# Two fused transformer blocks on one core: the second attention's steps taken one apart

## The reference

```python
# layer 1 of the second block
qkv = rmsnorm(x) @ w_qkv                      # 16 heads of 64, 4 key and 4 value heads
scores = einsum(q, k) / sqrt(64) + bias       # bias by distance, within 128 positions
probs = softmax(concat([scores, sink]))[..., :-1]
x = x + (probs @ v) @ w_o
# experts: per token and head, 16 of 128 keys on each of two sides, then 16 of the 256 pairs
sc = einsum((rmsnorm(x) @ w_q), subkeys)      # 8 heads, 2 sides
idx, g = best 16 pairs, softmax of their scores
h = x_norm . u_tab[idx];  a = g * gelu(h);  x = x + sum(a * v_tab[idx])
```

## Time and profile before

| what | value |
|---|---|
| median of three runs | 1950.23 us (1944.83 to 1954.89) |
| profiled execution | 1950.94 us, its span 1949.1 us |
| mean granted TensorE clock | 0.965 of full |
| TensorE busy | 1655.1 us (85%) |
| VectorE busy | 1049.2 us (54%) |
| ScalarE busy | 554.3 us (28%) |
| GpSimd busy | 587.3 us (30%) |
| moved by DMA | 639.39 MB, mean 328 GB/s |
| second expert loop | 1279.68 to 1949.10 us |

### The profile page before, as it was taken

How to read it: one execution, slowest core, us unless ns; L and a number is a source line. 1 busy time by engine, 2 the same in 40 slices (tenths; PEclk the granted TensorE clock), 3 DMA queues, 4 the chain that set the end, 5 groups by cost and what they waited for, 6 DMA issues and landing times.

```text
span 1949.1 us, 18676 instructions
## 1 busy us (share of the span) xinstructions
PE 1655.1 (85%) x6184; PEld 966.1 (50%) x6184; DVE 1049.2 (54%) x2676; ACT 554.3 (28%) x1664; POOL 587.3 (30%) x533
## 2 busy tenths in 40 slices
PE   7999999998779988787997868789898887777776
PEld 5888885885335544442543335544454443333232
DVE  2212202123676666676766643466677767677664
ACT  1211000101333433333333323243333343333432
POOL 1000000001344543344444420123344444444442
PEclk9999999999899999999999988789999999999999
DMA  8545241565999999999999982579999999999996
GB/s 215 130 129 171 100 165 65 195 226 196 392 409 400 421 417 418 417 421 420 408 420 407 418 316 80 198 297 405 418 418 420 421 421 420 393 421 418 420 422 274
DMA packets 149165, 639.39 MB, mean 328 GB/s; under 512 B 9923, under 2 KB 46803, under 8 KB 83276
## 3 DMA queue, kind: packets, MB, share of 16 engines
q0 software_dynamic: 75504, 543.01, 68.0%
q1 hardware_dynamic: 73564, 95.18, 14.8%
HBM read 637.05 MB, written 1.11 MB: 327 GB/s over the span
## 4 chain that ended last, share of the span: by engine, by line
PE 45%; DMA 31%; DVE 9%; issue 6%; ACT 4%; POOL 3%; another core or an unknown queue 0%; SPq 0%; DVEq 0%; POOLq 0%; ACTq 0%
DMA arena<-in_peer_uv,arena 30%; PE ps L1089 17%; PE ps L774 9%; DVE arena L1478 5%; PE ps L794 4%; POOL arena L522 3%; PE ps L762 3%; PE ps L805 2%; PE ps L968 2%; PE ps L753 1%; PE ps L1024 1%; ACT arena L664 1%; ACT arena L659 1%; PE ps L1044 1%; ACT arena L654 1%
## 5 line engine op out<-in xcount | busy, mean ns | idle before, releaser
L1089 PE MATMUL ps<-arena 128*128 128x512 f32 x2048 | 966.6, 617 | 221.3 <-ACT arena L664 220.6
L522 POOL DMA_INDIRECT arena<-in_peer_uv,arena x512 | 574.7, 1123 | 1134.9 <-PE ps L1089 597.6
L1478 DVE CUSTOM_DVE_ANT_0 arena<-xn,arena 128x1024 f32<-128x1024 f32 x512 | 622.4, 1225 | 374.9 <-DMA arena<-in_peer_uv,arena 358.6
L1089 PEld LDWEIGHTS ps<-arena 128*128 128x128 f32 x2048 | 380.7, 195 | 752.1 <-issue 391.7
L654 ACT ACTIVATE arena<-arena 128x2 f32<-128x2 f32 x256 | 52.1, 203 | 826.1 <-DVE arena L1478 826.1
L664 ACT ACTIVATE arena<-const,arena 128x128 f32<-128x128 f32 x512 | 177.6, 394 | 8.3
L774 PE MATMUL ps<-hT,wbuf 128*128 128x256 f32 x704 | 154.7, 382 | 2.6 <-DVE arena L1360 2.6
L774 PEld LDWEIGHTS ps<-hT,wbuf 128*128 128x128 f32 x704 | 134.6, 192 | 21.6 <-DVE arena L1360 3.0
L659 ACT ACTIVATE arena<-arena 128x1 f32<-128x1 f32 x512 | 123.3, 288 | 8.4
L968 PEld LDWEIGHTS ps<-hT,wbuf 128*128 128x128 f32 x768 | 94.0, 196 | 27.1 <-issue 26.1
L968 PE MATMUL ps<-hT,wbuf 128*128 128x128 f32 x768 | 94.7, 279 | 9.0 <-DMA wbuf<-in_peer_w_q 8.2
(11 more groups left out here) (157 smaller groups left out, 1179.6 us busy)
## 6 DMA issues: line engine op xcount, KB each, us to landing
wbuf<-in_w_in SPq DMA_DIRECT2D x36, 512.0 KB, 6.5
wbuf<-in_w_in SPq DMA_DIRECT2D x7, 2048.0 KB, 8.4
wbuf<-in_conv_w_in SPq DMA_DIRECT2D x6, 2048.0 KB, 7.8
wbuf<-in_peer_w_q SPq DMA_DIRECT2D x6, 2048.0 KB, 9.1
arena<-in_peer_uv,arena POOLq DMA_INDIRECT x512
wbuf<-in_attn_w_qkv SPq DMA_DIRECT2D x3, 2048.0 KB, 28.2
wbuf<-in_w_out SPq DMA_DIRECT2D x2, 2048.0 KB, 7.9
wbuf<-in_conv_w_out SPq DMA_DIRECT2D x2, 2048.0 KB, 7.8
```

Source lines behind the costliest of these rows:

```text
L522: pool.indirect_dma_start(ring[:, e % RING], None, A["peer_uv"], bass.IndirectOffsetOnAxis(ap=expert[:, unit % 2, e:e + 1], axis=0))\
L1089: last = mm(ps[t][:, s * 512:(s + 1) * 512], diag[:, e % RING], ring[:, e % RING, D + s * 512:D + (s + 1) * 512], start=False, stop=False, ...
L1478: last = nc.vector.tensor_tensor_reduce(out=ring[:, e % RING, 0:D], in0=xn[:, v // PEER_HEADS], in1=ring[:, e % RING, 0:D], scale=1.0, sca ...
```

## The change

In `attend` the steps that follow one another through the engines are taken one pair further apart: transposes and copy belong to the pair before the last, the product with the values to the one before, and so on; VectorE takes the row maxima ahead of the normalising. In each tile this makes 12 steps in place of 11.

```diff
+        w1 = at(4112, KC, 256)
...
             sp.dma_start(wo2, cols(A["attn_w_o_2"], 512, 512)).then_inc(wo2_landed, 16)
+            sp.dma_start(w1, cols(A["peer_w_q_2"][1], 0, 256)).then_inc(w1_landed, 16)
             load(*OUT_FILL, cols(A["attn_w_o_2"], 0, 512))
...
-            def keys_values_out(t):
+            def keys_out(t):
...
+            def values_out(t):
                 act.wait_ge(kv2_done, 2 * t + 2)
                 nc.scalar.activation(v2[:, t], psA[:, 512:768], ACT.Copy).then_inc(v2_copied, 1)
...
-                        keys_values_out(0)
+                        keys_out(0)
+                        values_out(0)
+                if layer == 0:
+                    nc.scalar.activation(small[:, 60:61], ident[:, 0:1], ACT.Exp)
                 act.wait_ge(x_added, (6, 10)[layer])
                 norm((4, 6)[layer], 1)
...
-            keys_values_out(1)
+            keys_out(1)
...
-                for p in range(8 + 1):
-                    if p > 0:
-                        copy_probs(8 * t + p - 1)
+                for p in range(8 + 2):
+                    if p >= 2:
+                        copy_probs(8 * t + p - 2)
+                    if t == 0 and p == 2:
+                        values_out(1)
...
-            def query_weights(layer, c):
-
+            def query_weights(layer, part):
+
+                c = PARTS[part][0]
+                if layer and part == 0:
+                    pe.wait_ge(w1_landed, 16)
+                    return w1
...
-                for p in range(8 + 3):
+                for p in range(8 + 4):
                     n = 8 * t + p
                     if p < 8:
                         scores_of(n)
-                    if 0 <= p - 1 < 8:
-                        turn_probs(n - 1)
-                    if p - 2 == 0:
+                    if t == 0 and p == 1:
+                        tile_values(1)
+                    if 0 <= p - 2 < 8:
+                        turn_probs(n - 2)
+                    if p == 3:
                         pe.wait_ge(v2_copied, 2)
-                    if 0 <= p - 2 < 8:
-                        times_v(n - 2)
-                    if t == 0 and p >= 3:
-                        pe.wait_ge(att2_copied, p - 2)
-                        if p == 3:
+                    if 0 <= p - 3 < 8:
+                        times_v(n - 3)
+                    if t == 0 and p >= 4:
+                        pe.wait_ge(att2_copied, p - 3)
+                        if p == 4:
                             pe.wait_ge(w_landed[OUT_FILL[0]], landed_value(*OUT_FILL))
                             pe.wait_ge(wo2_landed, 16)
-                        out_step(0, 0, p - 3)
-                        last = out_step(0, 1, p - 3)
-                        if p == 10:
+                        out_step(0, 0, p - 4)
+                        last = out_step(0, 1, p - 4)
+                        if p == 11:
                             last.then_inc(mixer_out, 1)
...
             tile_keys(1, 1)
-            tile_values(1)
...
             keys(1, 0)
+            for j in range(4):
+                tile_queries(psD[:, 512:1024], 1, 1, j)
             query_part(1, 1, 2)
             query_part(1, 1, 3)
-            for j in range(4):
-                tile_queries(psD[:, 512:1024], 1, 1, j)
             keys(1, 1)
...
-                for p in range(8 + 3):
+                for p in range(8 + 4):
                     n = 8 * t + p
-                    if 0 <= p - 3 < 8:
-                        heads_out(n - 3)
-                    if 0 <= p - 1 < 8:
-                        normalise(n - 1)
+                    if p >= 4:
+                        heads_out(n - 4)
                     if p < 8:
                         row_max(n, 0)
                         row_max(n, 1)
+                    if 0 <= p - 1 < 8:
+                        normalise(n - 1)
```

More of the change, by code:

```diff
@@ L283, in build @@
         wo2_landed = sem("wo2_landed")
+        w1_landed = sem("w1_landed")
         gain_loaded = sem("gain_loaded")
@@ L961, in queries @@
                 q = NPARTS * layer + part
-                w = query_weights(layer, c)
+                w = query_weights(layer, part)
                 products, _, _, _ = part_views(layer, part)
```

## The result

The changed kernel takes 1924.92 us (median of 4, 1922.47 to 1927.15) beside 1947.53 for the kernel before, whose four runs now lie between 1942.83 and 1954.89. These medians lie 22.6 us apart. The ratio on record is 0.9874, 95% interval 0.985 to 0.9897, which is 24.6 us of the forecast's 1950.23; 26.0 were forecast. Run once more beside two variants it gave 1925.41 beside 1949.38, 24.0 us less, ratio 0.988 (0.9865 to 0.9895).

What follows compares the result with a forecast made beforehand. It took the second expert loop as bound by transfers, so the attention tiles' ends decide its start. Gains of 3.7 + 9.8 + 12.5 = 26.0 us took the 1950.23 median to 1924, range 1919 to 1936.

Steps and rivals of the forecast that it cites:

- Before the first scores: Ahead of the first tile: scores start behind the key copy, at 1170.6 instead of 1173.55 behind the values product.
- The bias: First tile: its first half lands at 1173.4 instead of 1170.3 beside the new 1 MB load, unnoticed by TensorE.
- nearer 5 to 3: Queues ahead of the first tile: the trace's byte split, SP's 2.07 MB to POOL's 1.22 MB up to 1166.
- The output weights: First tile: load issued behind the values product lands at 1183.7, and TensorE stands 2.7 us at the first output step.
- First tile: Early scores and exp table against later output weights: tile ends at 1208.3 instead of 1212.0, gain 3.7 us, bounds 2.1 to 5.0.
- bound by its 3.73 and gains nothing: First tile: TensorE alone sets 3.73 us a pair of heads, so the new distance of steps gains nothing there.
- Between the tiles: Early query weights and moved query tiles shorten this stretch from 26.8 to 17.0 us: gain 9.8, bounds 7.6 to 10.4.
- Second tile: Steps one pair further apart shorten it from 32.0 us: gain 12.5, bounds 2 to 13.8.
- The 1.3 us that I subtracted: Second tile: reserve taken off the 13.8 us gain for uncounted handovers and a short fall of the clock.
- the lower clock: Rival: TensorE runs slow through the second tile, 3.3 us a pair, gain there 2, total 1935; chance 0.08.
- longer serial path: Rival: VectorE's row maxima ahead of normalising make a pair cost 5.8 us, total 1974; chance 0.03.
- Behind it: After the second tile: 12.6 MB moved 28 us after its first score, just when refill data would move; no loss.

Runs made afterwards that it cites:

- no_w1: Changed kernel without the early query weights, the first part's queries taking the late load again: 1938.16 us, ratio 0.9929.
- values_first: Changed kernel with the first tile's values product and its copy back ahead of the first scores: 1924.28 us, ratio 0.9878.
- w1_behind: values_first with the early query weights issued behind the output weights' load on SP's queue: 1922.53 us, ratio 0.9848.
- stage_alone: Kernel before with only the distance of the steps changed, in both tiles: 1935.63 us, ratio 0.9914.
- stage_undone: Changed kernel with the steps of both tiles back at the old distance and VectorE's old order: 1939.97 us, ratio 0.9949.
- no_move: Changed kernel with the second part's queries ahead of the query tiles again, early query weights kept: one execution of 1935.91 us.
- after_again: Changed kernel run once more beside two variants, nothing changed: 1925.41 us, ratio 0.988.
- after: The changed kernel itself, with every part of the change against the kernel before: 1924.92 us, ratio 0.9874.
- out_head: Changed kernel with three of eight pieces of the late output weights loaded early into the ring's free part: 1920.14 us, ratio 0.9849.
- w1_wide: Changed kernel with the early query weights in 2 KB rows where they fit, 1.97 MB in all: one execution of 1926.05 us.
- head_late_table: out_head without the early one-column exp, so the table load stands ahead of the first exp again: one execution of 1921.91 us.
- close_swapped: Changed kernel with the old distance on PE and ACT but VectorE's row maxima ahead of the normalising: 1956.54 us, ratio 1.002.

## Why the prediction was right

**Before the first scores: 2.95 forecast, 2.0 measured** in the changed kernel, 2.6 in its second run. The copy and the scores follow as said; what varies is the product for the keys in front of them, 6.8 us where it was 5.9. The lower clock is 10.2 us long in both kernels, but starts 2.8 us after the loop's end in the one and 4.5 in the other (3.3 in the second run, with 6.2 us for the product), so more of the product lies under it.

**The bias** was the wrong place to look. I put its first half at 3.1 us late and took that for hidden; it came 14.6 us after the loop's end and had come 14.7. The step that failed is the split read from the earlier trace rows, "nearer 5 to 3" in favour of SP's queue. That is a mean over a stretch in which POOL's queue had moved 7 packets up to 1161. With both at work, from 1163 to 1165 of the same trace:

```profile
q0 software_dynamic: 119, 0.49, 67.0%
q1 hardware_dynamic: 115, 0.24, 37.4%
```

Equal packets, 4 KB against 2 KB; against 1 KB the new load gets a fifth of the bytes. It is the load that is held up, and with it what stands behind it in its queue.

**The output weights: right number, wrong cause in part.** I had them at 28.1 from the loop's end, from the later issue alone, with 7.9 us for the load, and they came at 28.8. The later issue without the megabyte gives 27.7 and a stall of 2.4 us (no_w1). The megabyte in front with the early issue gives 29.0 and 3.6 (values_first). With neither the load lands at 26.6 (w1_behind). So each of the two is nearly enough by itself, and taking one away gains nothing in this tile. The prediction had only the first, and took the new load's effect on its own queue at nothing without a reason; that the number agreed all the same is luck.

**First tile: sum 3.7 forecast, 2.8 measured**, 1.7 in the second run, in which the clock was low for 6.8 us behind the stall, not 3.4. But the step "bound by its 3.73 and gains nothing" fell: stage_alone shortens this tile by 5.4. Before the change the tile begins with pairs at the second tile's serial rhythm and a low clock of 10.2 us; in stage_alone the low clock lasts 3.4. The rest of the change took the gain back, with the late output weights: 50.9 with the distance alone, 53.6 with everything, and 53.7 in stage_undone, where the weights come late and the distance is the old one. Behind the landing the sum holds: 23.7 us of TensorE's work and up to 1.7 for the clock were forecast, 24.8 measured. So the luck in this term is that of the landing.

**Between the tiles: 9.8 forecast, 10.2 measured**, from the same sum: 3.59 + 0.43 + 0.71 + 7.15 + 3.59 + 0.43 + 0.7 = 16.6. no_w1 gives 26.9 and no_move 21.5, where I had 3 for the move: it is 4.9, with the clock. This term is right by its mechanism.

**Second tile: 12.5 forecast, 12.6 measured,** 13.8 in the second run. The mechanism is right: stage_undone and the chains show it. The count without reserves, 18.2, is what two of the runs show at a clock of 1.00 (after_again and values_first). The 1.3 us that I subtracted stand for one of two disturbances in the others: the clock fell for 3.4 us in the first pairs (after, out_head, w1_wide), which I had named, or the unnamed gap of 1.8 to 1.9 us stood there (no_w1, w1_behind, head_late_table), which I had not. The rivals of the lower clock and the longer serial path didn't happen; the second one's price was shown by close_swapped, 3.5 to 4.9 a pair and not 5.8.

**Behind it.** The prediction's sum is off: 12.6 MB at 410 GB/s take 30.7 us, not 28. It didn't matter. The first refill went out 8.4 us after the tile's end, 8.9 before, released by TensorE in both. The loop gave back 1.1 us, and 3.2 in the second run, where the third refill went out 15.9 us behind the tile's end and not 14.3, with the clock at its lower level in between. The sum of the stages is 2.8 + 10.2 + 12.6 - 1.1 = 24.5, and 1.7 + 10.2 + 13.8 - 3.2 = 22.5 in the second run; the medians gave 22.6 and 24.0.

## What to carry to other kernels

Where a pair of units passes through several engines in turn, count the engines' occupation for one unit (here 1.6, 1.8 and 1.8 us) against its rhythm (3.63, or 3.17 at full clock): the difference is what one more step of distance gives. Move the step on all engines at once, for here VectorE's new order alone was slower than none. A load put early into a shared queue isn't free because it is needed late: ask what stands behind it in that queue, and how large its rows are beside those of the other queue. When a load lands late, look for more than one cause: here the late issue and the load in front were each nearly enough, and only taking both away ended the long stall. And after removing one wait in front of TensorE, look for the next load of the same buffer; here half of the gain needed the reordering of the work under it.

## What the runs showed of the hardware

Two DMA queues with work pending took turns packet by packet: 554 and 555 packets with 4 KB against 1 KB, 481 and 487 with 4 KB against 2 KB, 119 and 115 in the kernel before, so that the bytes went about 4 to 1 and 2 to 1. Within SP's queue a load issued at 1169.46 let the one ahead of it go first: up to 1173 all of the queue's packets had that one's 1 KB. At full clock a product of 32 matmul records of 128 columns took 3.59 us; behind a wait for its weights, with the lower clock at its start, it took 5.2 to 6.0.
